# A slot-by-slot schedule for the first expert tile, and three matmul pieces a slot instead of two

## The reference

```python
def peer_ffn(h, w_query, sub_keys, u_tab, v_tab):      # M=512 rows, H=8 heads, K=16
    q = (hf @ w_query).reshape(M, H, 2, 128)
    s = jnp.einsum('mhpc,hpnc->mhpn', q, sub_keys)
    top_s, top_i = lax.top_k(s, K)                     # 16 of 128 keys, twice a head
    cand_s = top_s[:, :, 0, :, None] + top_s[:, :, 1, None, :]
    cand_i = top_i[:, :, 0, :, None] * 128 + top_i[:, :, 1, None, :]
    best_s, best_c = lax.top_k(cand_s.reshape(M, H, K * K), K)
    ids = jnp.take_along_axis(cand_i.reshape(M, H, K * K), best_c, axis=-1)
    g = jax.nn.softmax(best_s, axis=-1)
    ...
        u = jnp.take(u_tab, idb, axis=0)               # 128 experts for each position
        v = jnp.take(v_tab, idb, axis=0)
        act = jax.nn.gelu(jnp.einsum('nkd,nd->nk', u, xb)) * gb
        return jnp.einsum('nk,nkd->nd', act, v)
```

## Time and profile before

| | us |
|---|---|
| median of 3 runs | 3024.39 (3023.88 to 3027.78) |
| the profiled execution | 3028.35 |
| its span, first to last instruction | 3026.6 |
| first gather issued | 213.4 |
| last gather issued | 3002.0 |
| DVE idle before dots, for gathers to land | 623.8 |
| PE idle before sums, for diagonals | 314.6 |

### The profile page before, as it was taken

How to read it: one execution, slowest core, us unless ns; L and a number is a source line. 1 busy time by engine, 2 the same in 40 slices (tenths; PEclk the granted TensorE clock), 3 DMA queues, 4 the chain that set the end, 5 groups by cost and what they waited for, 6 DMA issues and landing times.

```text
span 3026.6 us, 34984 instructions
## 1 busy us (share of the span) xinstructions
PE 2675.8 (88%) x11992; PEld 2188.5 (72%) x11992; DVE 2157.1 (71%) x6642; ACT 637.1 (21%) x1693; POOL 990.8 (33%) x1028
## 2 busy tenths in 40 slices
PE   8898999999998898989998898989999787777787
PEld 6786887777886676878887686768788565555555
DVE  1237867687688778778588778768678877678655
ACT  3221212711121215201111215201212110102001
POOL 0001333333333333333333333333333333333332
PEclk9998999999999999999999999999999999999999
DMA  5246999999999999999999999999999999999997
GB/s 189 94 175 239 414 412 424 383 422 426 426 405 410 408 426 418 415 426 423 426 410 412 412 427 419 409 427 416 427 419 391 421 426 418 426 418 406 425 423 332
DMA packets 166642, 1182.34 MB, mean 391 GB/s; under 512 B 19376, under 2 KB 19904, under 8 KB 23872
## 3 DMA queue, kind: packets, MB, share of 16 engines
q0 software_dynamic: 147456, 1073.81, 85.6%
q1 hardware_dynamic: 19008, 106.31, 9.0%
HBM read 1177.95 MB, written 2.10 MB: 390 GB/s over the span
## 4 chain that ended last, share of the span: by engine, by line
PE 53%; DMA 27%; DVE 10%; issue 7%; ACT 1%; POOL 0%; DVEq 0%; SPq 0%; ACTq 0%; POOLq 0%
PE main_bank L318 36%; DMA main_ring<-in_uv,main_idi 27%; PE main_bank L354 9%; PE main_bank L352 5%; DVE main_diagonal L301 2%; DVE main_ring L287 1%; PE main_bank L714 1%; DVE main_pick L199 1%; DVE main_hid L287 1%; DVE main_topi L162 1%; DVE main_work L154 1%; PE main_bank L522 1%; DVE main_pick L193 1%; DVE main_topi L156 1%; PE main_bank L730 1%
## 5 line engine op out<-in xcount | busy, mean ns | idle before, releaser
L318 PE MATMUL main_bank<-main_ring,main_diagonal 128*128 128x256 f32 (+1 forms) x8160 | 1996.0, 391 | 315.7 <-DVE main_diagonal L301 314.6
L318 PEld LDWEIGHTS main_bank<-main_ring,main_diagonal 128*128 128x128 f32 x8160 | 1536.1, 193 | 685.6 <-DVE main_diagonal L301 463.7
L287 DVE CUSTOM_DVE_ANT_0 main_ring<-main_ring,main_bank 128x1024 f32<-128x1024 f32 x1024 | 1247.7, 1219 | 634.8 <-DMA main_ring<-in_uv,main_idi 623.8
L270 POOL DMA_INDIRECT main_ring<-in_uv,main_idi x1024 | 990.6, 967 | 2011.9 <-PE main_bank L318 1764.2
L292 ACT ACTIVATE main_act_out<-main_hid 128x1 f32<-128x1 f32 x1024 | 206.9, 203 | 2201.9 <-DVE main_hid L287 2200.9
L301 DVE TENSOR_SCALAR main_diagonal<-main_ident,main_act_out,main_gate 128x128 f32<-128x128 f32 x1024 | 358.3, 350 | 33.1 <-PE main_bank L318 17.2
L354 PE MATMUL main_bank<-main_xT,main_w_block 128*128 128x256 f32 x1408 | 356.1, 381 | 4.3 <-ACT main_xT L387 4.3
L354 PEld LDWEIGHTS main_bank<-main_xT,main_w_block 128*128 128x128 f32 x1408 | 268.3, 191 | 41.5 <-ACT main_xT L387 4.9
L354 PE MATMUL main_bank<-main_xT_query,main_w_block 128*128 128x256 f32 x512 | 122.6, 380 | 0.9 <-ACT main_xT_query L387 0.9
L354 PEld LDWEIGHTS main_bank<-main_xT_query,main_w_block 128*128 128x128 f32 x512 | 97.3, 191 | 14.3 <-ACT main_xT_query L387 1.2
L292 ACT ACT_TABLE_LOAD x82 | 105.2, 1283 | 1.5
(11 more groups left out here) (187 smaller groups left out, 1205.5 us busy)
## 6 DMA issues: line engine op xcount, KB each, us to landing
main_w_block<-in_w_query SPq DMA_DIRECT2D x32, 1024.0 KB, 9.4
main_w_block<-in_w_ab SPq DMA_DIRECT2D x24, 1024.0 KB, 5.1
main_ring<-in_uv,main_idi POOLq DMA_INDIRECT x1024, 10.8
main_w_block<-in_w_c_in SPq DMA_DIRECT2D x16, 1024.0 KB, 9.4
main_w_block<-in_w_out SPq DMA_DIRECT2D x8, 1024.0 KB, 7.0
main_w_block<-in_w_c_out SPq DMA_DIRECT2D x8, 1024.0 KB, 9.5
main_att_bias<-in_att_bias SPq DMA_DIRECT2D x16, 256.0 KB, 5.9
main_resid<-in_x SPq DMA_DIRECT2D x2, 1024.0 KB, 7.6
```

The lines of the kernel that those rows point to most:

```text
L270: nc.gpsimd.indirect_dma_start(self.ring[n % self.bufs], None, self.uv[p // NT], bass.IndirectOffsetOnAxis(self.choice.idi[:, p % 2, k:k + ...
L287: self.nc.vector.tensor_tensor_reduce(out=row, in0=row, in1=self.ps[:, 6:8], scale=1.0, scalar=0.0, op0=ALU.mult, op1=ALU.add, accum_out=s ...
L318: last = self.nc.tensor.matmul(self.ps[:, 4 + at // T, at % T:at % T + wide], self.diagonal[:, n % DIAGS], self.ring[n % self.bufs][:, D + ...
```

## The change

Four things, in neutral words.
- Tile 0: PE computes four query blocks instead of eight before the slots, then transposes the second half's rows, and goes to slot 0. DVE chooses only pair 0 before slot 0 (and ranks head 2). The other four query blocks (64 pieces) stand in slots 2 to 23, the twelve input blocks in slots 24 to 87, and the rest of the choice in slots 8 to 50. The linear attention moves 21 to 26 slots later, the dilated attention from slot 84 to 88.
- Pace: `paced` and `ends` deal three pieces to a slot (`PACE`) in tile 0's pass and in the tail passes. A tail pass has its output pieces in slots 4 to 25 (before 4 to 35) and its query pieces in slots 32 to 74 (before 44 to 107).
- The choice in the tail passes (`PAIR_AT[0]`, `HEAD_AT[0]`) begins at slot 45 instead of 61, and heads no longer fall on the slots of `places`, `picked` or `numbers` of the pair before.
- For tiles 1 and 3 pair 0 moves from slot 18 to 52, pair 1 from 66 to 72 of the pass before.

```diff
-EARLY = 10
-PAIR_AT = ((65, 81, 97, 113), (18, 66, 130, 150))
-ATT_AT = 84
-def head_at(q, i):
-    return PAIR_AT[1][i // 2] + 3 * (i % 2) if q % 2 else 61 + 8 * i
+PAIR_AT = ((47, 60, 78, 98), (52, 72, 130, 150))
+HEAD_AT = ((45, 51, 58, 64, 76, 82, 96, 102), (52, 55, 72, 75, 130, 133, 150, 153))
+ATT_AT = 88
+PACE = 3
+def ends(first, b):
+    return first + (Weights.PIECES * (b + 1) - 1) // PACE
+def paced(k, first, count):
+    return range(max(0, PACE * (k - first)), max(0, min(count, PACE * (k - first + 1))))
...
         def _(dve):
-            for i in range(PH):
+            for i in range(3):
                 tail0.rank_dve(dve, 0, i)
-                if i % 2:
-                    choice.candidates(dve, i // 2)
...
-                if i in (2, 3, 4, 5, 6):
-                    experts.dot(dve, 0, 2 * i - 4)
-                    experts.dot(dve, 0, 2 * i - 3)
+            choice.gates(dve, 0, 0)
             for p in range(2 * NT):
-                for k in range(0 if p else EARLY, HK):
+                for k in range(HK):
...
+                        if k in (8, 15, 21, 26, 32):
+                            tail0.rank_dve(dve, 0, (8, 15, 21, 26, 32).index(k) + 3)
+                        if k in (10, 23, 35):
+                            choice.candidates(dve, k // 11 + (k == 10))
...
         def _(pe):
-            for i in range(PH):
+            for i in range(4):
                 tail0.pe_query(pe, 0, i)
-                if i == 6:
-                    experts.sum_rows(pe, 0, 0)
-                    experts.sum_rows(pe, 0, 1)
...
             mix0.turn_pe(pe, 1)
-            for x in range(2 * weights.PIECES):
-                mix0.in_piece(pe, 1, x)
...
+                        for x in paced(k, 2, 4 * weights.PIECES):
+                            tail0.pe_query_piece(pe, 0, 4 * weights.PIECES + x)
+                        for x in paced(k, 24, mix0.IN * weights.PIECES):
+                            mix0.in_piece(pe, 1, x)
...
-                        if 4 <= k < 36:
-                            for x in (2 * k - 8, 2 * k - 7):
-                                tail.pe_out_piece(pe, half, x, av if p > 1 else mix0.mixT[1])
-                        if 44 <= k < 108:
-                            for x in (2 * k - 88, 2 * k - 87):
-                                tail.pe_query_piece(pe, half, x)
+                        for x in paced(k, 4, 4 * weights.PIECES):
+                            tail.pe_out_piece(pe, half, x, av if p > 1 else mix0.mixT[1])
+                        for x in paced(k, 32, PH * weights.PIECES):
+                            tail.pe_query_piece(pe, half, x)
```

More of the change, by code:

```diff
@@ L1380, in _ @@
                         tail, half = tails[p]
-                        if k in (20, 28, 36, 44):
-                            tail.act_gains(act, half, (k - 20) // 8)
-                        if k == 46:
+                        for i in range(4):
+                            if k == ends(4, i) + 7:
+                                tail.act_gains(act, half, i)
+                        if k == 33:
                             tail.act_squares(act, half)
-                        if k == 50:
+                        if k == 36:
                             norms.root_mean(act, tail.n(half))
[L1387 to L1390, removed]
+                        for i in range(PH):
+                            if k == ends(32, i) + 3:
+                                tail.act_q(act, half, i)
+                            if k == ends(32, i) + 7:
+                                tail.act_scores(act, half, i)
                     if p in (2, 4):
@@ L1513, in _ @@
                         tail, half = tails[p]
-                        if k in (16, 24, 32, 40):
-                            tail.out_dve(dve, half, k // 8 - 2)
-                        if k == 48:
+                        for i in range(4):
+                            if k == ends(4, i) + 3:
+                                tail.out_dve(dve, half, i)
+                        if k == 35:
                             norms.mean_dve(dve, tail.n(half))
-                        if k == 52:
+                        if k == 38:
                             norms.scale_dve(dve, tail.n(half))
@@ L1576, in _ @@
             tail0.pe_turn(pe, 0, 3)
-            for i in range(PH):
+            for i in range(4):
                 tail0.pe_query(pe, 0, i)
-                if i == 6:
-                    experts.sum_rows(pe, 0, 0)
-                    experts.sum_rows(pe, 0, 1)
-            tail0.pe_scores(pe, 0, PH - 1)
-            experts.sum_rows(pe, 0, 2)
-            experts.sum_rows(pe, 0, 3)
-            pe.wait_ge(tail0.s_taken, PH)
+            pe.wait_ge(tail0.s_taken, 3)
+            pe.wait_ge(weights.taken, tail0.firsts[0] + 8)
@@ L1621, in _ @@
                             pe.wait_ge(mix1.gated, (half + 1) * RT)
[L1622 to L1630 removed]
+                        for x in paced(k, 4, 4 * weights.PIECES):
+                            tail.pe_out_piece(pe, half, x, av if p > 1 else mix0.mixT[1])
+                        for i in range(4):
+                            if k == ends(4, i) + 3:
+                                tail.pe_turn(pe, half, i)
+                        for x in paced(k, 32, PH * weights.PIECES):
+                            tail.pe_query_piece(pe, half, x)
+                        if k == 77:
                             tail.pe_scores(pe, half, PH - 1)
```

128 lines of the change are left out of this document (62 added, 66 removed).

## The result

The changed kernel takes **3052.6 us** (median of four, 3051.98 to 3053.41), against 3026.09 us (3023.88 to 3028.05) for the kernel before, median of four as well. The ratio is 1.0088, with a 95% interval of 1.0071 to 1.0105: it is slower, by 26.5 us. The forecast was 3045, in a range of 3016 to 3066. The profiled execution spans 3050.2 us (before 3026.6).

The account below looks back on a forecast made before the run. Tail passes were taken as filled by DMA, pass 0 nearly by PE. From the profiled 3028.35, -4.5 (start) +22 (tails) +3 (pairs) gave 3048.9, or 3045 us against the median; range 3016 to 3066.

Parts of the forecast that it names:

- Three are not: Slots with three pieces: PE needs 3.19 us against DMA's 2.91, so both cannot keep that pace.
- Part 2, the tails: Passes 1, 3 and 5 at three pieces a slot: +7.3 us a pass, +22 for three.
- the bank of 4.2 us a stretch: Tail passes: gathers banked while PE is late cover 1.7 slots, 4.2 us, in each of two stretches, -8.4 a pass.
- 2 us for lumps instead of 7: Tail passes' light slots: DVE's lumps cost 2 us instead of 7, since heads no longer share slots with another step.
- Part 1, the start: Pass 0: PE's loss falls from 24.6 to 20.1 us, a gain of 4.5, bounds -16 to +4.
- 8.8 us idle and 3.4 of slow clock: Pass 0's start: PE idles 8.8 us before the first diagonal, then loses 3.4 to half clock in slots 0 and 1.
- the later idle time: Pass 0's last two parts: PE's idle time stays as before, 7.9 us.
- Part 3, the moved pairs: Passes 2, 4 and 6: moved pairs stack on convolution steps, 1.5 us each in passes 2 and 4, +3, bounds -3 to +7.
- The ring covers the pace: Rival, chance 0.15: the bank is larger than thought, the tail passes stay at 350 us, kernel at 3023.
- Weights come late: Rival, chance 0.14: weights miss by 1 us on each of 36 tail blocks, kernel at 3081 us.
- Faster: Rival, chance 0.13: DMA alone sets the end, 28.6 us of unused DMA come back whole, tails stay, kernel at 2996.
- First gather at 213.4: Sign in pass 0: the first gather stays at 213.4 us, since all that comes before it is unchanged.

Follow-up runs that it names:

- e1: The changed kernel with the tail passes as before (two pieces a slot, old head slots); 3026.13 us, ratio 1.0000.
- e2: The kernel before with only the new tail passes (three pieces a slot, new slots of the choice of tiles 0 and 2); 3055.45 us, ratio 1.0085.
- e7: The changed kernel with e5's order, the tails of before with e6's heads, and e4's pairs; 3016.73 us, ratio 0.9967.
- e3: The changed kernel with projection pieces of passes 1, 3 and 5 cut to half width, slots and transfers unchanged; 3023.08 us, ratio 0.9989.
- e4: The changed kernel with pairs 0 and 1 of tiles 1 and 3 back at slots 18 and 66 in passes 2, 4, 6; 3047.53 us, ratio 1.0066.
- e10: The kernel before with three pieces a slot in the tail passes' output pieces alone (22 slots); 3029.93 us, ratio 1.0008.
- e11: The kernel before with three pieces a slot in the tail passes' query pieces alone (43 slots, from slot 44); 3057.32 us, ratio 1.0097.
- e6: The kernel before with heads 2, 4 and 6 of the tail passes three slots later, so none shares a slot with picked; 3025.44 us, ratio 0.9998.
- e8: As e7, but with five query blocks instead of four computed before the slots; 3012.11 us, ratio 0.9956.
- e5: The changed kernel with ACT's exponentials of pair 0 put behind the last query copy; 3053.96 us, ratio 1.0095.

## Why the prediction was right

The sign, the cause and the size held, by a sum whose terms were off in both directions. The parts as measured: start about -9 (forecast -4.5); tails +23 to +25 by the passes and +26.5 to +28 by the medians of e1 and e2 (forecast +22); moved pairs +5 to +12, with 9 in between from e1 and e7 (forecast +3). With 9 for the pairs that is 23 to 28 together; the medians give 26.5, the forecast's sum was 20.5. That the start gained more than was forecast while the other two cost more brought the sum nearer than its terms were, and that was luck.

**What bounds.** "Three are not" held to the digit: 3.02 us from sum to sum, PE 133.00 of 133.00, DMA at 384 GB/s where under 410 was forecast. e3 shows the ground of it by taking PE's load and leaving the rest.

**Part 2, the tails.** Forecast +22. e4 differs from the kernel before in the start and the tails only: passes 1 and 2 +7.0, pass 3 +9.4, pass 5 +7.0, together 23. e2 shows 25 in the passes and 28 in the medians. The sign for pass 1 was wrong by itself (369 where 356 to 360 was named): I didn't look where SyncE's loads hang, and they came with the earlier scores. This changes no sum. Of the two corrections inside the term, the bank of 4.2 us a stretch fits e10 but not e11. The gain of 5 us a pass from spread heads (2 us for lumps instead of 7) is not shown: at two pieces a slot e6 finds it to be nothing. What gave 7 us above 343 in a tail pass of before is therefore open, and the 22 rests in part on two corrections that could offset each other. Without them the sum would have been 364.1 - 350.4 = 13.7 us a pass, 41 for three, so the runs show that something like them exists, but not which.

**Part 1, the start.** Forecast -4.5, measured about -9 (e7 against e6; the passes 0 with the new start, without e8's, average 391.6, those with the old one, 401.1; the 12.6 between the two profiles above is at the edge, since 403.45 is the longest of the old ones). Two steps failed, and a term was mis-sized. The scores at 213.89 were read as those of head 2, but they are head 3's, behind the query block after. Head 2's are these, in PE's timeline of the kernel before:

```profile
206.09 1.05 PE L522 MATMUL main_bank<-main_keys,main_q 128*128 128x128 f32 x8
```

So PE stops 7.8 us earlier than the forecast had it. And ACT's exponentials stood ahead of a query copy (e5). Against that I had counted 8.8 us idle and 3.4 of slow clock before and in slots 0 and 1. The rows give, within the pass, 1.5 + 5.4 = 6.9 us idle; transposes in 3.67 for 1.91, 1.8 slow; three sums in 8.10 for 3 x 1.73 = 5.2, 2.9 slow: 11.6 for 12.2. The term that was mis-sized is the later idle time, put at 7.9 us: PE's windows leave 0.00 and 0.90. In this pass's slots of three pieces DVE's work no longer came last, so PE had nothing to wait for. Of the 390.85 us of the pass 11.6 + 0.9 = 12.5 are then loss, where 24.6 had been counted for the kernel before and 20.1 forecast.

**Part 3, the moved pairs.** Forecast +3, bounds -3 to +7. e4 shows 5 us in the medians and 8.5 + 4.0 in the passes. The mechanism was the named one, the stack of choice and convolution; its price was taken from a single pile-up at one slot, while here two heads and three steps of the convolution share 20 us, and again in slots 80 to 95, and the idle time of pass 2 did not absorb them. Here the lumps cost what the gathers lost (0.2 to 0.3 us each over 32 slots of a pass, part of it given back by the slots that grew lighter), not what PE waited (42.9 us for 42.5).

**The rivals.** *The ring covers the pace*: true for 22 slots (e10), not for 43 (e11). *Weights come late*: in pass 1 PE waits for diagonals and for no weights,

```profile
PE main_bank L318 <- DVE main_diagonal L301: 39.7, 35, 2.9
```

(waits of the changed kernel, 609.85 to 979.05: us in total, times, longest), and e3 used its blocks faster still. *Faster*: the 28.6 us of unused DMA were nearly all put to use (share 0.97 for 0.67), and 9 us came out, since PE's 383 us stood above DMA's 358 as feared. The Trainium skill (Perfetto Trace Analysis, section Optimization Strategy) speaks for interleaving regimes with different bounds. In this case the new start, taken by itself, pays, but only by what PE, which is nearly full in both stretches, had idle or lost to its clock.

**The signs.** First gather at 213.4: it was at 219.0, for a reason outside the change (below). Pass 0 ended 7.0 us earlier, at 609.85, in place of 5; it was not over 15 shorter. No wait for weights.

## What to carry to other kernels

When two engines are near balance, work each slot at both prices: a pace that fits both (2.70 and 2.76 us here) and one piece more (3.19 and 2.91) differ by a regime, and the loss is not given back when the second stage is bound by the other. Filling a stretch in which DMA is idle helps only as far as the engine that is full there had gaps of its own. Moving a wait gives nothing (e5); putting work that will be needed on the binding engine into it may (e8, 4.6 us between medians, not clear of noise).

## What the runs showed of the hardware

The first gather came between 213.4 and 219.4 us in the profiled executions, though the program's chain of work up to it is the same: 219.2 and 219.4 in two kernels with the old start, 213.5 in e5 with the new one. The windows of 130 to 166 us, the kernel before and then the changed one:

```profile
130.00:166.00 36.00, 28.14 (x143) 23.66 (x143) 9.07 (x11) 6.72 (x13) 0.00 (x0) 0.86 0.23 81
```

```profile
130.00:166.00 36.00, 28.13 (x129) 22.23 (x128) 9.08 (x11) 7.78 (x14) 0.00 (x0) 0.72 0.17 59
```

PE is busy for the same time, 28.1 of 36 us, but the mean granted clock is 0.86 in one and 0.72 in the other, and fewer matmuls are recorded (129 for 143). The engine has gaps in this stretch in both. In the twelve profiled executions a first gather at 213.4 or 213.5 us goes with a clock of 0.86 there, 216.4 to 217.7 with 0.81, and 217.7 to 219.4 with 0.72. The clock is not all of it: the two executions that stand at 217.7 with 0.72 (e4, e11) moved 226 and 227 GB/s between 11 and 35 us, the three behind 219.0 moved 197 to 201. Both differ from execution to execution and move everything behind by up to 6 us, a fifth of a percent, about as much as parts 1 and 3 of this change are worth; so the parts were read from the lengths of passes beside the medians.
